# Six attention units issued between the slots of a reordered projection, the recurrence as one scan, the output product in two halves

## What is computed

```python
h = x @ w_in[l] + b_in[l]
lru_x, lru_gate, q, kc_raw, vc_raw, ks_, vs_, kw_, vw_, gts = jnp.split(h, offsets, axis=-1)
y_lru = _rg_lru(lru_x, lru_gate, ...)      # causal conv, r,i gates, h_t = a_t h_{t-1} + u_t, times gelu(gate)
kc = _compress(kv(kc_raw), ...)            # windows of 32 tokens, stride 16, a small two-layer network
vc = _compress(kv(vc_raw), ...)
y_nsa = _nsa(q, kc, vc, ks_, vs_, kw_, vw_, gts)   # compressed + selected + window attention, 8 heads, gated
mix = jnp.concatenate([_rms_norm(y_lru, g1), _rms_norm(y_nsa, g2)], axis=-1) @ w_out[l]
x = _layer_norm(ALPHA * x + mix, ln1_g[l], ln1_b[l])
```

## Time and profile before

| | us |
|---|---|
| median of 3 runs | 3439.72 |
| lowest, highest | 3438.03, 3439.92 |
| the profiled execution, its own time | 3440.78 |
| its span in the trace | 3439.0 |
| nsa stage of layer 0, first projection matmul to first matmul of the next stage | 1248.1 to 1444.15 |
| nsa stage of layer 1, the same | 2340.3 to 2538.8 |
| PE busy over the span | 3208.5 (93%) |
| DVE busy, ACT busy | 2257.0 (66%), 1466.3 (43%) |

### The profile page before, as it was taken

One profiled execution on the slowest core, in us unless ns is written; L12 is line 12 of the kernel. 1 busy time (PEld: TensorE's weight loads), 2 busy tenths in 40 slices (PEclk: granted clock), 3 DMA queues, 4 the chain that ended last, 5 costly groups with the idle time before them and its releaser, 6 DMA issues.

```text
span 3439.0 us, 46624 instructions
## 1 busy us (share of the span) xinstructions
PE 3208.5 (93%) x15800; PEld 2692.0 (78%) x15800; DVE 2257.0 (66%) x4522; ACT 1466.3 (43%) x2151; POOL 162.1 (5%) x297
## 2 busy tenths in 40 slices
PE   4988999999899997899899999999799989999998
PEld 3677888767788886788788888887678978888887
DVE  3636777462777737199966666664538986666666
ACT  1325666432566624213334444443411334444444
POOL 1100000010000000041000000000005000000000
PEclk9978999998999998899999999999799999999999
DMA  6745888471688842242365555553134245555553
GB/s 213 251 148 210 298 298 294 164 251 57 245 295 296 297 176 66 69 141 87 95 193 188 185 189 188 184 190 143 37 106 141 69 132 192 184 190 188 185 190 125
DMA packets 167140, 614.71 MB, mean 179 GB/s; under 512 B 18752, under 2 KB 18784, under 8 KB 166096
## 3 DMA queue, kind: packets, MB, share of 16 engines
q1 hardware_dynamic: 151632, 551.62, 47.6%
q0 software_dynamic: 15360, 61.16, 5.2%
HBM read 611.66 MB, written 1.05 MB: 178 GB/s over the span
## 4 chain that ended last, share of the span: by engine, by line
PE 80%; DVE 11%; DMA 4%; ACT 3%; DVEq 2%; issue 1%; POOL 0%; ACTq 0%; POOLq 0%
PE PS L1473 13%; PE PS L1475 13%; PE PS L1474 13%; PE PS L1970 10%; PE PS L1501 7%; PE PS L1971 5%; PE PS L1959 4%; PE PS L1940 3%; DMA arena<-in_w_ada 3%; PE PS L1513 2%; PE PS L1523 1%; DVE arena L868 1%; DVE arena L1348 1%; DVE arena L1349 1%; PE PS L1486 1%
## 5 line engine op out<-in xcount | busy, mean ns | idle before, releaser
L1970 PE MATMUL PS<-x_lh,w_hi 128*128 128x512 f32 x1536 | 548.1, 397 | 0.0
L892 DVE TENSOR_TENSOR w_lo<-arena,w_hi 128x1024 fp32r<-128x1024 f32 x448 | 530.3, 1220 | 1.9 <-ACT w_hi L530 1.9
L530 ACT ACTIVATE w_hi<-arena 128x1024 fp32r<-128x1024 f32 x448 | 450.7, 1048 | 120.3 <-DMA arena<-in_v_t 78.2
L1971 PE MATMUL PS<-x_lh,w_lo 128*128 128x256 f32 x1536 | 430.9, 281 | 0.0
L1473 PE MATMUL PS<-w_hi,pw_hi 128*128 128x512 f32 x1024 | 407.9, 398 | 22.9 <-DVE w_lo L892 22.4
L1475 PE MATMUL PS<-w_hi,pw_lo 128*128 128x512 f32 x1024 | 403.3, 394 | 0.0
L1474 PE MATMUL PS<-w_lo,pw_hi 128*128 128x512 f32 x1024 | 401.4, 392 | 0.0
L1970 PEld LDWEIGHTS PS<-x_lh,w_hi 128*128 128x128 f32 x1536 | 288.6, 188 | 69.0
L1119 DVE TENSOR_TENSOR gu_lo<-raw,gu_hi 128x1024 fp32r<-128x1024 f32 x256 | 297.7, 1221 | 30.1 <-ACT gu_hi L621 29.7
L1971 PEld LDWEIGHTS PS<-x_lh,w_lo 128*128 128x128 f32 x1536 | 289.9, 189 | 7.4
L1501 PE MATMUL PS<-x,arena 128*128 128x256 f32 x1152 | 260.5, 387 | 11.4 <-ACT x L687 10.3
(11 more groups left out here) (404 smaller groups left out, 5204.4 us busy)
## 6 DMA issues: line engine op xcount, KB each, us to landing
raw<-in_w_gu SPq DMA_DIRECT2D x256, 512.0 KB, 5.3
arena<-in_u_t SPq DMA_DIRECT2D x256, 512.0 KB, 4.5
arena<-in_v_t SPq DMA_DIRECT2D x256, 512.0 KB, 3.6
arena<-in_w SPq DMA_DIRECT2D x152, 512.0 KB, 3.5
raw<-in_w_down SPq DMA_DIRECT2D x128, 512.0 KB, 5.5
arena<-in_w_ada POOLq DMA_DIRECT2D x96, 512.0 KB, 5.3
arena<-in_tab POOLq DMA_DIRECT2D x2, 1664.0 KB, 15.2
arena<-in_x POOLq DMA_DIRECT2D x2, 1632.0 KB, 10.4
```

The lines of the kernel that those rows point to most:

```text
L530: A(w_hi[:, m % RING], ring[:, m % RING], ACT.Copy).then_inc(S["hi_done"], 1)
L892: V.tensor_tensor(w_lo[:, m % RING], ring[:, m % RING], w_hi[:, m % RING].bitcast(F32), ALU.subtract)\
L1970: mm(PS[:, 4 + j % 4, :], hi, x_lh[:, :, k], start=k == 0, stop=False)
L1971: last = mm(PS[:, 4 + j % 4, T:2 * T], lo, x_hi[:, k], start=False, stop=k == KT - 1)
```

## The change

- **Slot order.** The projection's pairs are computed as 0, 1, 4, 5, 8, 9, 6, 7, 2, 3: queries and keys come ahead of the compressed branch's input and of the gate, which is last. SP loads the slots in that order. The pairs use PSUM banks 0 and 1 only, `gates()` banks 4 to 7, `values()` and the compressed branch 2 and 3.
- **Units.** Six units of 1024 scores each, in banks 4 and 5 or 6 and 7 in turn: the 256-key units are split by the parity of the head. Each has its own buffer for the shares. Their `scores` and `turn` stand between the slots of the projection from slot 9 on, as do the compressed branch's pieces. `gates()` and `values()` both stand after slot 5.
- **Recurrence.** The doubling loop becomes one `tensor_tensor_scan` over the four tiles laid end to end (4 x 256); the first coefficient of each tile is set to 0, so that no state passes from one to the next.
- **Gate.** Its gelu is read out last, half of it straight from PSUM.
- **Output product.** The multiply into `mix` signals after each half. PE runs the first half (k = 0 to 3, the recurrence's part) of output slots 0 to 3 while the attention part's norm is being made, then the rest.
- ACT's and DVE's programs are reordered to match; the convolution starts after pair 0.

The core of the diff:

```diff
 W2_IN, W2_OUT, W2_Q = 20, 8, 16
+P_ORDER = [0, 1, 4, 5, 8, 9, 6, 7, 2, 3]
+W2_ORDER = [*(2 * j + q for j in P_ORDER for q in range(2)), *range(W2_IN, W2_IN + W2_OUT)]
+OUT_BANK = (4, 5, 0, 1)
 EARLY, EARLY_1 = 32, 16
 GDEEP = 6
 PEER_SLOTS = 2 * PK - EARLY
@@ -254,8 +257,9 @@
         N["mix"] = arena[:, 5120:7168].rearrange("p (a b) -> p a b", b=T)
...
+        UNITS = [(0, 0, 0), (0, 1, 0), (0, 1, 1), (1, 0, 0), (1, 1, 0), (1, 1, 1)]
+        NUN = len(UNITS)
+
+        def unit_heads(u):
+
+            br, t, par = UNITS[u]
+            return NH // (t + 1), P * (t + 1), 3 * NH * br + (NH + NH * par if t else 0)
+
+        def unit_bank(u):
+            return 4 + 2 * (u % 2)
 
...
+                act.wait_ge(S["tm_mm"], l + 1)
+                A(N["vtm"], PS[:, 2:4, 0:4 * HD], ACT.Copy)
+                A(N["gt"], PS[:, 2:4, 4 * HD:TMW], ACT.Sigmoid).then_inc(S["tm_ev"], 1)
...
-                evac(5)
+                evac(3)
+                evac(4)
...
+                evac(5)
                 exps(1)
                 turned(0)
                 exps(2)
+                evac(6)
                 turned(1)
+                evac(7)
+                turned(2)
                 exps(3)
-                turned(2)
+                act.wait_ge(S["cmp_mm"], 2 * l + 1)
+                for q, name in ((0, "b1k"), (1, "b1v")):
+                    last = A(N["gel"][0:HD, q], PS[0:HD, 2 + q, 0:2 * NC], ACT.Gelu_apprx_tanh, bias=c2(l, name)[0:HD])
+                last.then_inc(S["cmp_ev"], 1)
+                evac(8)
+                exps(4)
                 turned(3)
+                act.wait_ge(S["cmp_mm"], 2 * l + 2)
+                A(N["kc"], PS[:, 2, 0:2 * NC], ACT.Identity, bias=c2(l, "b2k"))
+                for j in range(4):
+                    last = A(N["vcz"][32 * j:32 * j + 32, j], PS[32 * j:32 * j + 32, 3, 0:HD], ACT.Copy)
+                last.then_inc(S["cmp_ev"], 1)
+                turned(4)
+                exps(5)
+                act.wait_ge(S["cs_max"], l + 1)
+                A(N["cs"][:, :, :, 0:NC], N["cs"][:, :, :, 0:NC], ACT.Exp).then_inc(S["cs_exp"], 1)
+                A(N["gg"][:, 0:2], N["p"][:, 4:6], ACT.Gelu_apprx_tanh)
+                act.wait_ge(S["slot_done"], n0 + W2_IN)
+                for q in range(2):
+                    last = A(N["gg"][:, 2 + q], PS[:, 1, T * q:T * q + T], ACT.Gelu_apprx_tanh, bias=c2(l, "b_in", 6 + q, 1))
+                last.then_inc(S["pair_evac"], 1)
+                act.wait_ge(S["cc_mm"], 2 * l + 2)
+                A(N["ct"], PS[:, 2, :].rearrange("p (a b) -> p a b", b=P), ACT.Copy).then_inc(S["ct_ev"], 1)
+                turned(5)
+                act.wait_ge(S["ylru_ok"], l + 1)
+                A(N["sq"][:, 0:4], N["u"], ACT.Square).then_inc(S["g_sq"], 1)
                 heads_out(0)
+                rms(0, 3)
                 heads_out(1).then_inc(S["g_sq"], 1)
-                rms(1, 7)
+                rms(1, 2)
                 layer_norm(l, 0)
...
+                V.memset(N["a0"][:, :, 0:1], 0.0)
                 V.tensor_scalar(N["a1"], N["u"], -1.0, 1.0, ALU.mult, ALU.add)
...
+                dve.drain()
+                fl = lambda v: v.rearrange("p a b -> p (a b)")
+                V.tensor_tensor_scan(fl(N["xc"]), fl(N["a0"]), fl(N["u"]), 0.0, ALU.mult, ALU.add)
+                shares(0)
+                highest(1)
+                shares(1)
+                highest(2)
+                shares(2)
+                windows(0, "pos_k")
+                highest(3)
+                windows(1, "pos_v")
+                shares(3)
+                highest(4)
                 dve.wait_ge(S["cmp_ev"], 2 * l + 1)
                 for j in range(4):
...
+                dve.wait_ge(S["pair_evac"], p0 + 10)
+                V.tensor_tensor(N["u"], N["xc"], N["gg"], ALU.mult).then_inc(S["ylru_ok"], 1)
...
+                last.then_inc(S["mix2_ok"], 1)
                 dve.wait_ge(S["g_rs"], 2 * l + 2)
...
-                for j in pairs(n0, p0, W2_IN // 2, x, ("nsa", l)):
-                    if j == 3:
-                        gates()
-                    if j == 5:
-                        values()
-                    if j == 8:
-                        compressed()
...
+                    br, t, par = UNITS[u]
+                    nh, nk, _ = unit_heads(u)
+                    b = unit_bank(u)
+                    pe.wait_ge(S["pair_evac"], p0 + 5 + br)
+                    if u < 2:
+                        pe.wait_ge(S["ri_ev"], l + 1)
+                    else:
+                        pe.wait_ge(S["att_tev"], NUN * l + u - 1)
+                    for hp in range(nh):
+                        hh = 2 * hp + par if t else 2 * (hp % 4) + hp // 4
+                        o, j, g = HD * (hh % 2), hh // 2, hh // REP
+                        c0 = hp * nk
...
+                    b = unit_bank(u)
+                    pe.wait_ge(S["p_ok"], NUN * l + u + 1)
+                    for i in range(NH):
+                        last = nc.tensor.transpose(PS[:, b + i // 4, P * (i % 4):P * (i % 4) + P], N["sv"][u][:, P * i:P * i + P], ident)
...
+                def out_half(i, c):
+                    n = n0 + W2_IN + i
+                    wait_slot(pe, n)
+                    for k in range(4 * c, 4 * c + 4):
+                        last = mm(PS[:, OUT_BANK[i // 2], T * (i % 2):T * (i % 2) + T], ring[:, n % RING, P * k:P * k + P], N["mix"][:, k],
+                                  start=k == 0 and i % 2 == 0, stop=k == KT - 1, skip_group_check=True)
+                    if c:
+                        last.then_inc(S["slot_done"], 1)
+                for i in range(W2_IN):
+                    j, q = i // 2, i % 2
+                    if q == 0 and p0 + j >= 2:
+                        pe.wait_ge(S["pair_evac"], p0 + j - 1)
+                    wait_slot(pe, n0 + i)
+                    for k in range(KT):
+                        if i == 0:
+                            wait_x(pe, ("nsa", l), k)
+                        last = mm(PS[:, j % 2, T * q:T * q + T], ring[:, (n0 + i) % RING, P * k:P * k + P], x[:, k],
+                                  start=k == 0, stop=k == KT - 1)
+                    last.then_inc(S["slot_done"], 1)
+                    if i == 5:
+                        gates()
+                        values()
+                    if i == 9:
+                        scores(0)
+                    if i == 10:
+                        scores(1)
+                    if i == 11:
+                        turn(0)
+                    if i == 12:
+                        scores(2)
+                    if i == 13:
+                        turn(1)
+                    if i == 14:
+                        scores(3)
+                    if i == 15:
+                        turn(2)
+                    if i == 16:
+                        compressed()
+                        scores(4)
+                    if i == 17:
+                        turn(3)
+                        compressed_2()
+                    if i == 18:
+                        turn(4)
+                        scores(5)
+                        compressed_scores()
+                compressed_turn()
+                pe.wait_ge(S["ct_ev"], l + 1)
+                pe.wait_ge(S["att_tev"], NUN * l + 4)
+                heads(0, (0, 1))
+                turn(5)
+                pe.wait_ge(S["pair_evac"], p0 + 10)
+                heads(1, (0,))
...
+                pe.wait_ge(S["att_tev"], NUN * l + 6)
                 heads(1, (1,))
-                sums(1, 7)
-                pe.wait_ge(S["mix2_ok"], l + 1)
-                for j in pairs(n0 + W2_IN, p0 + 10, 4, N["mix"]):
-                    if j:
-                        means(l, 0, j - 1)
+                pe.wait_ge(S["mix2_ok"], 2 * l + 1)
+                out_half(0, 0)
+                out_half(1, 0)
+                sums(1, 2)
+                out_half(2, 0)
+                out_half(3, 0)
+                pe.wait_ge(S["mix2_ok"], 2 * l + 2)
+                for i in range(W2_OUT):
+                    if i >= RING:
+                        out_half(i, 0)
+                    out_half(i, 1)
+                    if i % 2 and i > 1:
+                        means(l, 0, i // 2 - 1)
                 means(l, 0, 3)
```

311 lines of the change are left out of this document (117 added, 194 removed).

## The result

The changed kernel takes **3387.69 us** (median of 4 runs, 3382.82 to 3392.95) beside 3439.01 for the kernel before (4 runs, 3438.03 to 3439.92): a ratio of **0.9852, 95% interval 0.9837 to 0.9868**. Forecast was 3387. The profiled execution took 3392.95 us, its span is 3391.2.

The account below looks back on a forecast made before the run. No engine bounds it, but one dependent chain behind a PE-full projection; 28.7 us earlier minus 2.5 gives 26.2 a layer, 52.4 in both, so the 3439.0 span becomes 3386.6 and the time 3387 us; range 3378 to 3407.

Parts of the forecast that it names:

- The layout of three queues: PE, ACT and DVE programs laid side by side: layer 0's first output matmul at 1373.2 us, 28.7 us earlier.
- slack of 0.3: Room at unit 4's turn, after ACT's table load and pair 8's copy; no wait of PE was forecast there.
- The scan: The recurrence's scan on DVE: taken as 1.22 us, bounded by 1.22 and 6.55; at 6.55 a layer loses 4.5 us.
- The output product: From first output matmul to last mean, 33.6 us against 31.2 before; 2.5 us more for a sum and a wait.
- as they are: Output product's first 64 records, 15.77 us at a clock of 0.57, were priced as unchanged.
- its low side: Low side of 3381 to 3394 us: output product starts at full clock, 2 us a layer; layer 1 transposes speed up.
- All this is work that the kernel did before: PE's work in the new order, up to the output product, is unchanged work adding up to 116.4 us.
- fall behind small pieces: Rival, chance 0.18: clock falls behind narrow matmuls between slots and in the tail; 9 us a layer, 3405 us.
- Late units: Rival, chance 0.12: PE stands at turns whose shares are late; 7.5 us a layer, 3402 us.
- A scan with a price for each element's dependence: Rival, chance 0.03: DVE's scan pays per element, break-even 27 ns; at 50 ns an element 3486 us.
- the change doesn't do what it says: Rival, chance 0.02: `pair_evac` copies throttle PE, units and slots alternate without overlap; within 0.2% of before, 3440.
- I price all of it at the full clock: Pricing rule for PE's 116.4 us: full clock, since only 1 to 3 us stands between pieces.

Follow-up runs that it names:

- tripled scan: Changed kernel with the scan executed three times, the two extra into scratch; 3393.80 us, ratio 0.9871 to the kernel before.
- compressed first: Changed kernel with the compressed branch's scores ahead of unit 5's, ScalarE and VectorE steps moved to match; 3383.51 us, ratio 0.9833 to the kernel before.
- wait filled: Changed kernel with 12 extra unread matrix products where TensorE waits ahead of the compressed turn; 3385.75 us, ratio 0.9850 to the kernel before.
- the last experiment: Changed kernel with compressed scores ahead of unit 5's, recurrence's sums of squares earlier, and heads dealt so row halves and banks alternate; 3371.43 us, ratio 0.9807 to before.
- changed again: The changed kernel itself, unaltered, measured in a second job; 3377.67 us, ratio 0.9828 to the kernel before.
- units behind: Changed kernel with the six units' scores, maxima, exponentials, shares and turns moved behind the projection; 3456.07 us, ratio 1.0057 to the kernel before.
- fitted fill: Changed kernel with 6 extra unread products ahead of the compressed turn and 4 ahead of the output product; 3385.08 us, ratio 0.9846 to before.

## Why the prediction was right, step by step

**The time.** 3387 forecast, 3387.69 measured; 52.4 us of gain forecast, 51.3 measured. Part of the closeness is chance: the code around the two stages alone moves by more than the difference, as the table of stages shows. The stages are the fairer test: 26.2 us each forecast, 25.4 and 25.2 measured.

**The layout of three queues** held. Last slot done 108.1 us after the start by it, 108.95 in layer 0 and 110.8 in layer 1, which began with a longer wait for transfers. First output matmul 124.9 by it, 128.1 and 130.8 measured: 3 and 6 us late. The waits are not the reason. In the projection of layer 0 they sum to 2.7 us, as forecast, though spread otherwise (0.50 at slot 5 for 1.2, and 0.60 at the turn of unit 4, whose slack of 0.3 was thus not there); in the tail they were 2.95, 0.69 and 1.98 us against 2.9, 0.7 and 2.2. What was late is work: the first five slots took 18.1 us and not 17.3, the first heads lost 1.7 us to the lower clock, and the heads without that come to 8.1 us and not 7.4. In layer 1, where the clock was also low at the start, the first five slots took 19.3 us, the turn of unit 4 waited 0.96, and the lower clock cost the first heads 2.2 us and the compressed turn 0.5. The room at unit 0, 0.9 as I expected it for the tripled scan, came out as 0.8 and 1.2.

**The scan** took 2.29 us, and 1.22 was taken. Its bounds of 1.22 and 6.55 held, the choice between them was off by 1.1 us. That cost room and no time: the turn of unit 0 waited for nothing. The Trainium skill (DVE: opcode table, instruction layouts, handler registers and perf-mode slots, section 6) says half throughput; four such rows of 2.26 to 2.29 us against 1.22 for a pass of the same size agree.

**The output product** from its first matmul to the last mean's end: 33.6 us forecast, 34.0 measured. The added sum and its wait of 0.49 came as said. The 31.2 us for before did not: in its trace it is 33.2 us, 2 of them the slow start at a clock of 0.57. Such a start was to stay "as they are"; it went away. That this is because PE now comes from dense heads is not shown: in layer 1 of compressed first and of wait filled the slow start came back behind the same heads. From the first output matmul to the next stage it is 0.8 us longer in layer 0, not 2.5, and 0.3 shorter in layer 1. This error in my favour met the 3 and 6 us of the layout against me: 26.2 and 24.9 us earlier at the first output matmul where 28.7 were forecast, and 25.4 and 25.2 a stage. The forecast had named it as its low side.

**"All this is work that the kernel did before"** is the step that failed, without costing the forecast anything. 1.75 us for four heads over 256 keys is half of the 3.42 us of the earlier trace rows, and that row ran mostly at the lower clock (0.57 over it) with alternating halves of the rows. Cutting the unit by parity doubled the time of a matmul at a given clock (3.75 us for eight, 3.78 for sixteen), and the upper clock halved it again. Two errors cancelled and gave 1.75 against the measured 1.99. Priced correctly, the change adds some 4.5 us of TensorE work a layer (four units at 1.99 for 1.13, two at 1.71 for 1.16); the last experiment dealt the heads out again and was 3.7 and 4.1 us a stage shorter.

**The rivals.** The clock did fall behind small pieces, but in each trace of the changed kernel only at one place a layer, and at a cost of 1.5 to 2.6 us, not 9. The slots between the units kept their 3.6 to 3.7 us, except the last one in one stage (5.41 us, changed again). Late units came to 0.6 and 1.0 us a layer, not 7.5. A scan with a price for each element's dependence was refuted by its row: 2.2 ns an element, with 27 needed to break even. That the change doesn't do what it says was refuted by PE's busy share, 106.25 of 108.95 us.

**What decided it.** The new order and the scan need each other: 2.8 and 5.8 us a stage alone, 25.3 together. And part of the gain is the clock: the big scores and the big turns of the earlier trace rows (3.42 and 3.65 us) ran at half rate in a tail full of waits, and scores and turns run at the full rate between slots. The forecast had this only as a pricing rule ("I price all of it at the full clock"), but the run with units behind suggests how much hangs on it: its layout, priced at the full clock, missed 19 us of whole time.

## What to carry to other kernels

When a chain through several engines stands behind a stretch in which one engine is full, price the laid-over order with a layout of each engine's queue, and look for the step whose slack is smallest; a long pass on the other engine must go first, or the interleaving only moves the wait. Check at which clock the row was taken that you price with, and which rows of the array neighbouring matmuls use: splitting work by the dimension that made them alternate can double its cost. Where whole times move by 10 us from run to run in code nobody touched, compare the stage that changed.

## What the runs showed of the hardware that I had not expected

- TENSOR_TENSOR_SCAN over 128x1024 f32 takes 2.29 us, and 2.2 from one to the next, against 1.22 for a two-operand pass of that size.
- Matmuls with a contraction of 64 on alternating halves of the rows, into different banks, take 1.13 us for eight of 256 columns at the upper clock, 1.99 when all are on one half; at the lower clock 3.78 for sixteen against 3.75 for eight.
- The granted clock can fall while PE is 100% busy: 9.00 of 9.00 us with a mean of 0.81 in the fitted fill. Filling a gap moved the fall or took it away; fills fitted to the gaps took 1.5 to 1.6 us off a stage, one twice too long took nothing off.
- The same program's first 1240 us differ by 13 us between two of its traces, with the clock of single stretches at 0.72 in one and 0.82 in the other (850 to 900 us).
